# Recurrent branch of a two-block network: the gates' products as 64 by 64 blocks in the quarters of the matrix array

## The reference

```python
LRU_WIDTH, LRU_BLOCKS = 1024, 16         # 64 channels in a block
def rg_lru(u, w_rg, b_rg, w_ig, b_ig, lru_lambda):
    ub = uf.reshape(B, S, LRU_BLOCKS, LRU_BLOCK_DIM)
    r = sigmoid(einsum('bshi,hij->bshj', ub, w_rg).reshape(B, S, LRU_WIDTH) + b_rg)
    i = sigmoid(einsum('bshi,hij->bshj', ub, w_ig).reshape(B, S, LRU_WIDTH) + b_ig)
    log_a = -LRU_C * r * softplus(-lru_lambda)
    a = exp(log_a)
    xin = sqrt(-expm1(2.0 * log_a)) * (i * uf)
    # h_t = a_t * h_(t-1) + xin_t along the positions
...
u = causal_depthwise_conv(u, conv_w, conv_b)
y_b = (rg_lru(u, ...) * silu(g_lru)) @ w_pb
```

## Time and profile before

| | us |
|---|---|
| median of three runs | 2720.86 |
| their range | 2720.74 to 2721.09 |
| the profiled execution | 2721.44 |
| its span, first to last instruction | 2720.1 |

### The profile page before, as it was taken

How to read it: one execution, slowest core, us unless ns; L and a number is a source line. 1 busy time by engine, 2 the same in 40 slices (tenths; PEclk the granted TensorE clock), 3 DMA queues, 4 the chain that set the end, 5 groups by cost and what they waited for, 6 DMA issues and landing times.

```text
span 2720.1 us, 35231 instructions
## 1 busy us (share of the span) xinstructions
PE 2682.1 (99%) x14497; PEld 2203.2 (81%) x14497; DVE 1634.8 (60%) x3269; ACT 1026.0 (38%) x1751; POOL 14.8 (1%) x43
## 2 busy tenths in 40 slices
PE   8999999999999999999999999999999999999999
PEld 5788888889888888766888889888889666888888
DVE  6766555356767556777876746763346777633334
ACT  4652332435222244565422224322234565422223
POOL 1000000000000000000000000000000000000000
PEclk9999999999999999999999999999999999999999
DMA  8255333133655334400555524543223410232331
GB/s 252 80 175 171 111 101 117 63 109 109 214 188 186 108 106 123 128 32 32 186 186 186 186 89 143 187 143 103 93 93 117 140 55 32 65 107 93 97 101 66
DMA packets 345353, 331.41 MB, mean 122 GB/s; under 512 B 11363, under 2 KB 334695, under 8 KB 345193
## 3 DMA queue, kind: packets, MB, share of 16 engines
q1 hardware_dynamic: 344820, 328.62, 38.8%
q10 hardware_dynamic: 372, 0.55, 0.1%
HBM read 320.74 MB, written 2.10 MB: 119 GB/s over the span
## 4 chain that ended last, share of the span: by engine, by line
PE 93%; DVE 4%; ACT 1%; SPq 1%; DMA 0%; issue 0%; DVEq 0%
PE bank L542 26%; PE bank L544 26%; PE bank L543 26%; PE bank L584 3%; PE bank L2405 2%; PE bank L570 2%; PE bank L572 2%; PE bank L571 2%; PE bank L2434 1%; PE bank L1385 1%; PE bank L1375 1%; PE bank L2039 1%; DVE w_lo L510 0%; DMA mw<-in_w_mod 0%; SPq L815 0%; PE bank L2053 0%
## 5 line engine op out<-in xcount | busy, mean ns | idle before, releaser
L542 PE MATMUL bank<-h_lo,w_hi 128*128 128x512 f32 (+1 forms) x2448 | 923.0, 377 | 3.6 <-DVE h_lo L709 2.2
L544 PE MATMUL bank<-h_hi,w_lo 128*128 128x512 f32 (+1 forms) x2448 | 900.3, 368 | 0.0
L543 PE MATMUL bank<-h_hi,w_hi 128*128 128x512 f32 (+1 forms) x2448 | 898.5, 367 | 0.0
L510 DVE TENSOR_TENSOR w_lo<-raw,w_hi 128x1024 fp32r<-128x1024 f32 (+1 forms) x422 | 491.0, 1200 | 313.9 <-ACT w_hi L504 313.8
L504 ACT ACTIVATE w_hi<-raw 128x1024 fp32r<-128x1024 f32 (+1 forms) x422 | 421.5, 1034 | 343.5 <-PE bank L544 326.5
L542 PEld LDWEIGHTS bank<-h_lo,w_hi 128*128 128x128 f32 x2448 | 461.3, 188 | 87.2 <-issue 7.7
L544 PEld LDWEIGHTS bank<-h_hi,w_lo 128*128 128x128 f32 x2448 | 460.6, 188 | 77.9
L543 PEld LDWEIGHTS bank<-h_hi,w_hi 128*128 128x128 f32 x2448 | 461.8, 189 | 76.1 <-issue 4.3
L542 PE MATMUL bank<-a_lo,w_hi 128*128 128x512 f32 (+1 forms) x1056 | 390.9, 370 | 0.0
L544 PE MATMUL bank<-a_hi,w_lo 128*128 128x512 f32 (+1 forms) x1056 | 384.5, 364 | 0.0
L543 PE MATMUL bank<-a_hi,w_hi 128*128 128x512 f32 (+1 forms) x1056 | 384.1, 364 | 0.0
(11 more groups left out here) (313 smaller groups left out, 2529.2 us busy)
## 6 DMA issues: line engine op xcount, KB each, us to landing
swf<-in_w_ada SPq DMA_DIRECT2D x60, 1024.0 KB, 7.9
raw<-in_ffn_w_gate SPq DMA_DIRECT2D x44, 1024.0 KB, 5.3
raw<-in_ffn_w_up SPq DMA_DIRECT2D x44, 1024.0 KB, 5.3
raw<-in_w_in SPq DMA_DIRECT2D x40, 1024.0 KB, 5.1
raw<-in_ffn_w_down SPq DMA_DIRECT2D x32, 1024.0 KB, 5.2
raw<-in_w_in SPq DMA_DIRECT2D x34, 512.0 KB, 5.1
raw<-in_ffn_w_down SPq DMA_DIRECT2D x16, 768.0 KB, 4.5
mw<-in_w_mod SPq DMA_DIRECT2D x8, 1024.0 KB, 11.9
```

The lines of the kernel that those rows point to most:

```text
L510: nc.vector.tensor_tensor(o, r, half(w_his[place_of[i]], i, h)[0].bitcast(F32), ALU.subtract).then_inc(*w_lo.up((i, h)))
L542: nc.tensor.matmul(o, w1, al, start=start, stop=False)
L543: nc.tensor.matmul(o, w1, ah, start=False, stop=False)
L544: return nc.tensor.matmul(o, w2, ah, start=False, stop=stop)
```

## The change

The gates' products no longer use zero blocks. For each block of 128 channels `pe_gates_of` now issues four matmuls with 64 by 64 weights. The first gate's two halves go from partitions 0 to 63 of `uc` to partitions 0 to 63 of bank `br`, and from 64 to 127 to 64 to 127. The input gate's two halves are crossed: from 0 to 63 of `uc` to 64 to 127 of bank `bi`, and from 64 to 127 to 0 to 63. So each of the four uses another quarter of the array. ScalarE puts the input gate's halves back: its Tanh of `bi` becomes two instructions of 64 partitions each, which read one half of the bank and write the other half of `ii`. The input gate's bias is loaded with its halves exchanged, in two transfers in place of one. GpSimd's two clearings and SyncE's wait for them are gone.

```diff
@@ load_vectors
+            if name == "b_ig":
+                for hh in range(2):
+                    queue.dma_start(vs[g][r0:r0 + n, 64 - hh * 64:128 - hh * 64], ap[:, hh * 64:hh * 64 + 64]).then_inc(
+                        *ld_v[g].up(g, 16))
@@ sp_start
-        sp.wait_ge(pool, "wg0")
@@ pool_start
-        v.memset(wrg[:, :], 0.0).then_inc(*pool.up("wg"))
-        v.memset(wig[:, :], 0.0).then_inc(*pool.up("wg0"))
@@ pe_gates_of
-        nc.tensor.matmul(br[:, :], wrg[:, c * 128:c * 128 + 128], uc[c % 4][:, :], start=True, stop=True).then_inc(
-            *pe.up(("br", c)))
-        nc.tensor.matmul(bi[:, :], wig[:, c * 128:c * 128 + 128], uc[c % 4][:, :], start=True, stop=True).then_inc(
-            *pe.up(("bi", c)))
+        half = (slice(0, 64), slice(64, 128))
+        for a, r in enumerate(half):
+            w = slice(c * 128 + 64 * a, c * 128 + 64 * a + 64)
+            m = nc.tensor.matmul(br[r, :], wrg[r, w], uc[c % 4][r, :], start=True, stop=True)
+        m.then_inc(*pe.up(("br", c)))
+        for a, r in enumerate(half):
+            w = slice(c * 128 + 64 * a, c * 128 + 64 * a + 64)
+            m = nc.tensor.matmul(bi[half[1 - a], :], wig[r, w], uc[c % 4][r, :], start=True, stop=True)
+        m.then_inc(*pe.up(("bi", c)))
@@ act_gates_of
-            nc.scalar.activation(ii[c % 4][:, :], ps.of(("bi", c))[:, :], use(ACT.Tanh), scale=0.5,
-                                 bias=half_b[:, 8 + c:9 + c]).then_inc(*act.up(("i", c), lets=("bi", c)))
+            for a in range(2):
+                r, o = slice(64 - 64 * a, 128 - 64 * a), slice(64 * a, 64 * a + 64)
+                m = nc.scalar.activation(ii[c % 4][o, :], ps.of(("bi", c))[r, :], use(ACT.Tanh), scale=0.5,
+                                         bias=half_b[r, 8 + c:9 + c])
+                m.then_inc(*act.up(("i", c, a) if a == 0 else ("i", c), lets=("bi", c) if a else None))
```

More of the change, by code:

```diff
@@ L801, in load_vectors @@
         for name, ap, n in groups[g]:
-            if name.startswith("sub_g"):
+            if name == "b_ig":
+                for hh in range(2):
+                    queue.dma_start(vs[g][r0:r0 + n, 64 - hh * 64:128 - hh * 64], ap[:, hh * 64:hh * 64 + 64]).then_inc(
+                        *ld_v[g].up(g, 16))
+            elif name.startswith("sub_g"):
                 for hh in range(2):
```

## The result

| | before | after |
|---|---|---|
| median of 20 runs each, us | 2720.98 | 2726.99 |
| lowest to highest | 2719.78 to 2721.95 | 2723.94 to 2729.07 |
| the profiled execution, its span | 2721.44, 2720.1 | 2725.88, 2724.4 |

The ratio after / before is 1.0022 [1.0016, 1.0028]: slower by 6.0 us. The bound of 0.2% (5.4 us) that the forecast named lies inside the interval. The forecast was 2720.8 with a range up to 2724.8, so the time lies outside it.

The account below looks back on a forecast made before the run. TensorE, busy 99% of the span, was taken to bound the kernel. Gates -3.4, waits for the ScalarE-VectorE loop +3.15, start +0.2 sum to -0.05 us: from 2720.86 to 2720.8 us, range 2718.2 to 2724.8.

Parts of the forecast that it names:

- Gates, -3.4 us: TensorE's gate matmuls: all four quarters run together, 1.29 us a block in place of 1.71, 3.4 us gained in eight blocks.
- rivals of pairs: At the gates, two quarters run at once and two behind them: 2.13 us a block, 2724.5 us in all; chance 0.10.
- banks that exclude each other: Two halves of one bank can't be written together: 2.99 us a block, 2731.3 in all; 0.11, shared with stricter orders.
- ScalarE, +1.14 a pair: Two more half Tanhs, 0.57 us each, make ScalarE's work for each pair of blocks 1.14 us longer.
- What lies behind block 1: After the gates of blocks 0 and 1, ScalarE's 4.13 us wait for TensorE swallows the added 1.14 us.
- Block 6, 1.0 us of wait: At block 6's gates TensorE waits about 1.0 us for the bank of block 4's input gate, read until 131.65.
- Mb1: A later TensorE unit: its first half's weights `w_lo` are done at 152.05, so it starts at most 0.94 us sooner.
- pb0: A later TensorE unit: its second half's `w_lo` is done at 169.06, needed at 169.31, leaving 0.25 us of the gain.
- Start, +0.2: The input gate's bias in two transfers adds one SyncE issue ahead of a weight transfer on the chain: 0.2 us later.

Follow-up runs that it names:

- Vectors later: The changed kernel with three transposes of vectors moved behind a later unit on TensorE, VectorE's part behind the decay of blocks 0 and 1: 2726.26 us.
- the room: The changed kernel with ScalarE's list block by block, weights formed earlier, units reordered, auxiliary banks for one: 2716.74 us; same moves without quarters and halves: 2719.23 us.

## Why the prediction was wrong

- **Gates, -3.4 us.** Right in kind, a little too small. All four quarters run together, 1.22 us a block in place of the 1.29 forecast, some 4.0 us in eight blocks. The first pass lasts 0.48 and not 0.53. The rivals of pairs and of banks that exclude each other fall: the halves of `br`, one bank and two row halves, start side by side (the row of 67.73 holds both). The Trainium skill ("TensorEngine Tiling (Array Packing)", Restrictions and Gotchas) says that different row tiles can't be at one PSUM bank at once; for these two, which also write different partitions of the bank, the rows do not agree.
- **ScalarE, +1.14 a pair.** A term that was mis-sized. It was worked out as two more instructions of 0.57, and the pair takes 4.26 in place of 2.28, +1.98. The row of 64 partitions gave the duration of one instruction and said nothing of the distance to the next; that distance is what overlapping made short. The Trainium skill ("ScalarE: Activation LUTs", What ACT_TABLE_LOAD costs) gives about 280 ns and 0.833 ns a value for an instruction with a bias operand, which makes an estimate of 706 ns for 512 values, and an overlap of about 93 ns between neighbours. The step of 0.71 without overlap agrees with the first. The overlap here is 0.14, and it goes where the start partition changes.
- **What lies behind block 1.** The step that failed. The forecast said that blocks 0 and 1 cost nothing because ScalarE waits 4.13 us afterwards. That is ScalarE's own slack. TensorE waits for ScalarE there in the meantime, at three transposes right behind block 1's gates whose banks have to be read first, and the trace of before showed it: 0.26 us of wait at 76.82. Those three rows were passed over, since the list of what TensorE would meet began at block 6. They cost 1.5 us, and the slow stretch behind them 1.6. "Vectors later" moves these three, with VectorE's part of them, and nothing else, and its trace has 3.2 us of lag at 1164 us in place of 5.9, though its median doesn't show it.
- **Block 6, 1.0 us of wait.** It was 2.41. It follows from the points above: ScalarE ends block 4's `ii` at 136.27 where 131.65 was forecast. Of those 4.6 us, some 3.5 are TensorE's own lag by then (the transposes and the slow clock behind them, +2.7 in place of -0.8), 0.8 the mis-sized pair before, 0.3 the half in hand.
- **The clock.** In no term of the sum. Two slow stretches of 3.4 us, 3.2 us together, are over half of the 6.0. The forecast held that a wait costs what it lasts.
- **Mb1 and pb0.** Mb1's start was bounded by 0.94 us sooner than before, and it came 5.2 later: 3.7 of lag that TensorE brought there and the rest at the place itself, the same lateness handed on. pb0's second tile was to start within 0.5 us of 169.31. That point was named as the test, and it fell: 175.19 is 5.9 later, and the short wait there is for a bank that ScalarE's merge gate reads, not for `w_lo`.
- **Start, +0.2.** Within the scatter of zero.

What stays open: what decides whether the clock falls at a wait. In all the traces, between 66 and 180 us, it fell at or just behind waits of 2.41, 2.52, 2.69, 2.75, 3.40, 3.67 us and longer, and behind 1.72 in three pieces. It didn't behind single waits up to 1.95 and behind 1.12 in two pieces. Behind the 2.00 us at the transpose near 1167 us it fell in 10 of the 16 traces. The slow stretches were never brought about or kept away by themselves, only together with the waits. Nor is it settled what the median of the changed kernel has beyond its traces (6.0 and 4.3 us in two comparisons, 4.4 and 4.0 in the profiled executions).

## What to carry to other kernels

An instruction added to a helper engine is to be priced by the distance to its neighbours in the new order and not by its duration, and every consumer that waits for its bank or tile is to be listed from the first one on, those that wait a quarter of a microsecond today above all. Slack of the helper behind the place doesn't cover a wait of the bounding engine at the place. Before a saving on the bounding engine is counted, move work so that what it waits for next has room: here the quarters with their halves lost 4 to 6 us without the room, and with it they won 2.5.

## What the hardware showed that was not expected

- Four 64 by 64 float32 matmuls in the four quarters start within 0.02 us of each other. All eight passes take 1.22 us with both changes of mode, against 1.71 for two full matmuls (four passes) and 2.06 with two quarters at a time.
- ScalarE's step between activations of 512 values is 0.57 us while the start partitions stay, and 0.71 when either changes; the instruction after pays too.
- Silu then Tanh needs one table load, Tanh then Silu two, 1.28 us each.
- Between 66 and 180 us each wait of TensorE of 2.4 us or more came with 3.4 to 6.8 us of granted clock at 0.50, which costs 1.5 us or more on top of it.
